# Expert phase: all column blocks from fetched token rows, none fetched for empty places

## What is computed

```python
scores = sigmoid(xt @ router_w)                # 384 tokens x 64 experts
idx = top 8 of 64, within 4 of 8 groups        # TOP_K = 8
w = scores[idx] / sum * 2.5
out = sum over the 8 chosen e of w_e * (silu(x @ w1[e]) * (x @ w3[e])) @ w2[e]
```

## Time and profile before

| | |
|---|---|
| median of 3 runs | 1401.55 us (1399.53 to 1402.01) |
| profiled execution | 1400.54 us |
| its span | 1398.7 us |
| mean granted TensorE clock | 0.997 |
| PE busy | 1363.8 us (98%) |
| DVE, ACT, POOL busy | 600.3, 392.6, 309.2 us |
| DMA traffic | 321.97 MB |
| expert weights, 198 loads of 1 MB | 207.6 MB |

### The profile page before, as it was taken

How to read it: one execution, slowest core, us unless ns; L and a number is a source line. 1 busy time by engine, 2 the same in 40 slices (tenths; PEclk the granted TensorE clock), 3 DMA queues, 4 the chain that set the end, 5 groups by cost and what they waited for, 6 DMA issues and landing times.

```text
span 1398.7 us, 20850 instructions
## 1 busy us (share of the span) xinstructions
PE 1363.8 (98%) x7808; PEld 958.6 (69%) x7808; DVE 600.3 (43%) x1347; ACT 392.6 (28%) x773; POOL 309.2 (22%) x247
## 2 busy tenths in 40 slices
PE   7999999999999999999999999999999999999996
PEld 2695898899988996788988875444455444444453
DVE  3467451885545477433321375232223322332224
ACT  3232221322554364323431241221121211221122
POOL 0431232243134552554233000000000000000001
PEclk9999999999999999999999999999999999999998
DMA  9540423123212428611135336899999999999992
GB/s 364 201 136 0 136 91 120 53 99 101 81 60 91 135 91 321 237 61 41 52 106 170 129 126 279 359 418 418 419 418 419 420 419 419 420 418 419 419 420 119
DMA packets 107376, 321.97 MB, mean 230 GB/s; under 512 B 9776, under 2 KB 69936, under 8 KB 78768
## 3 DMA queue, kind: packets, MB, share of 16 engines
q1 hardware_dynamic: 98416, 307.45, 56.6%
q0 software_dynamic: 2560, 10.49, 1.9%
q10 hardware_dynamic: 6336, 3.15, 0.8%
HBM read 316.93 MB, written 4.13 MB: 230 GB/s over the span
## 4 chain that ended last, share of the span: by engine, by line
PE 85%; DMA 10%; DVE 2%; ACT 1%; issue 1%; POOL 1%; SPq 0%; POOLq 0%; DVEq 0%
PE banks L647 21%; PE banks L614 20%; PE banks L2938 12%; PE banks L2989 7%; DMA w<-in_exp_w 7%; PE banks L2840 6%; PE banks L1054 3%; PE banks L2825 3%; PE banks L621 2%; PE banks L1207 1%; PE banks L886 1%; DMA ring<-in_ada_w 1%; PE banks L2833 1%; PE banks L766 1%; PE banks L698 1%
## 5 line engine op out<-in xcount | busy, mean ns | idle before, releaser
L2938 PE MATMUL banks<-w,xg 128*64 128x512 f32 (+1 forms) x1312 | 236.2, 594 | 0.9 <-DMA w<-in_exp_w 0.6
L2938 PEld LDWEIGHTS banks<-w,xg 128*64 128x64 f32 (+1 forms) x1312 | 72.0, 126 | 150.3 <-issue 124.0
L647 PE MATMUL banks<-hT,ring 128*128 128x192 f32 x792 | 137.6, 326 | 0.0
L3312 POOL DMA_INDIRECT fetched<-token_rows,row_of_place x32 | 30.4, 951 | 480.1 <-DVE row_of_place L3120 479.8
L647 PEld LDWEIGHTS banks<-hT,ring 128*128 128x128 f32 x792 | 129.6, 190 | 1.7 <-DMA ring<-in_w_in 0.4
L2989 PE MATMUL banks<-w,hidT 128*64 128x512 f32 (+1 forms) x656 | 122.0, 600 | 0.0
L2840 PE MATMUL banks<-y,selT 128*128 128x512 f32 x384 | 112.6, 415 | 0.0
L647 PE MATMUL banks<-x,ring 128*128 128x192 f32 x528 | 96.9, 327 | 0.9 <-ACT late L1383 0.9
L647 PE MATMUL banks<-x,combos 128*128 128x192 f32 x528 | 96.6, 326 | 0.0
L3130 DVE SCALAR_TENSOR_TENSOR hid<-banks,gslot,sil 128x256 f32<-128x256 f32 x33 | 16.0, 484 | 177.6 <-ACT sil L3024 176.9
L2840 PEld LDWEIGHTS banks<-y,selT 128*128 128x128 f32 x384 | 66.2, 189 | 35.4 <-issue 26.2
(11 more groups left out here) (483 smaller groups left out, 2055.7 us busy)
## 6 DMA issues: line engine op xcount, KB each, us to landing
w<-in_exp_w SPq DMA_DIRECT2D x198, 1024.0 KB, 17.2
ring<-in_w_in SPq DMA_DIRECT2D x46, 1024.0 KB, 5.2
ring<-in_ada_w SPq DMA_DIRECT2D x24, 1024.0 KB, 6.8
ring<-in_w_branch SPq DMA_DIRECT2D x8, 1024.0 KB, 6.2
ring<-in_w_out SPq DMA_DIRECT2D x4, 1024.0 KB, 6.2
arena<-in_sh_w SPq DMA_DIRECT2D x3, 1024.0 KB, 8.3
x<-in_x_sample SPq DMA_DIRECT2D x4, 512.0 KB, 8.7
arena<-in_t_last_layer SPq DMA_DIRECT2D x1, 1024.0 KB, 8.5
```

The source lines that it names most:

```text
L647: last = mm(out, lhsT=w[:, k, :], rhs=tokens[:, k, :], start=start and k == 0, stop=k == KD // 2 - 1, skip_group_check=not start)
L2938: ins = mm(ps[lo:hi, :], lhsT=xg[:, k, a_ * P + lo:a_ * P + hi], rhs=w13[:, a_, u, :, k, :], start=k == 0, stop=k == KD - 1)
L3312: nc.gpsimd.indirect_dma_start(fetched[:, a_, :], None, rows[:, :], bass.IndirectOffsetOnAxis(ap=row_of_place[:, 2 * a_:2 * a_ + 1], axis= ...
```

## The change

All eight column blocks come from fetched rows in every round but the first preparation, in which the first two blocks are still gathered. `token_rows`, `fetched` and a fetch are 1024 columns (4096 bytes a row). An empty place now has row 512, which is beyond the table's 384 rows: `turn_by` carries row - 512 and `rows_of_pair` adds 512. The indirect DMA is given a bound of 383 and told that a number beyond it is no error, so it fetches nothing for such a place. `fetched` is cleared once before the first fetch. `whole_rows` is one tile of 128 x 1024: GpSimd's add of a tile waits for the store of the one before, the third also for the planner's first table (X 2). TensorE waits for the fetches ahead of turned block 0, with 8 of 12 scatter matmuls (in the first round 12) before block 1, and one between each pair of the others.

```diff
-        sb("fetched", P, 2, D - FROM_ROWS),
+        sb("fetched", P, 2, D),
-        sb("whole_rows", P, NT, D - FROM_ROWS),
+        sb("whole_rows", P, D),
...
-    rows = nc.dram_tensor("token_rows", (T, D - FROM_ROWS), F32, kind="Internal").ap()
+    rows = nc.dram_tensor("token_rows", (T, D), F32, kind="Internal").ap()
...
-            if hi == 12:
+            if lo < hi == 12:
                 ins.then_inc(s_scat, 1)
...
                 elif a_:
-                    close_bank(gather(0, open_bank(GATHERS[0])))
-                    out = open_bank(GATHERS[1])
-                    gather(1, out, (0,))
-                    parts = (6, 10, 11, 12) if first else (6, 7, 10, 12)
+                    parts = (6, 12, 12, 12) if first else (8, 9, 10, 11)
                     if first:
+                        close_bank(gather(0, open_bank(GATHERS[0])))
                         scatter(1 - a_, *parts[0:2])
+                    else:
+                        scatter(1 - a_, 6, parts[0])
                     pe.wait_ge(s_fetched, 32 * q + 32)
-                    close_bank(turn_rows(1, out, (1,)))
                     if not first:
+                        close_bank(turn_rows(0, open_bank(GATHERS[0])))
                         scatter(1 - a_, *parts[0:2])
+                    close_bank(turn_rows(1, open_bank(GATHERS[1])))
+                    scatter(1 - a_, *parts[1:3])
                     close_bank(turn_rows(2, open_bank(GATHERS[2])))
-                    scatter(1 - a_, *parts[1:3])
+                    scatter(1 - a_, *parts[2:4])
                     close_bank(turn_rows(3, open_bank(GATHERS[3])))
                 if add:
-                    scatter(1 - a_, parts[2] if a_ else 6, 12)
+                    scatter(1 - a_, parts[3] if a_ else 6, 12)
...
-                    act.wait_ge(s_stored, 16 * NT)
+                    act.wait_ge(s_row_stored[NT - 1], 16)
...
-            v.tensor_copy(row_of_place[...], row_sum[...].to_broadcast([P, 2])).then_inc(s_rows, 1)
+            ts(row_of_place[...], row_sum[...].to_broadcast([P, 2]), float(NOWHERE), None, ALU.add
+               ).then_inc(s_rows, 1)
...
         for t in range(NT):
-            nc.gpsimd.tensor_tensor(whole_rows[:, t, :], h2[HI][:, t, FROM_ROWS:]..., h2[LO][:, t, FROM_ROWS:]..., ALU.add)
+            if t:
+                pool.wait_ge(s_row_stored[t - 1], 16)
+            if t == 2:
+                pool.wait_ge(s_read["dve"], read(0, "dve", ("X", 0, 2), "first"))
+            nc.gpsimd.tensor_tensor(whole_rows[:, :], h2[HI][:, t, :]..., h2[LO][:, t, :]..., ALU.add)
-        pool.wait_ge(s_stored, 16 * NT)
+        pool.wait_ge(s_filled, 1)
+        nc.gpsimd.memset(fetched[:, :, :], 0.0).then_inc(s_blank, 1)
+        pool.wait_ge(s_row_stored[NT - 1], 16)
+        pool.wait_ge(s_blank, 1)
...
-                    bass.IndirectOffsetOnAxis(ap=row_of_place[:, 2 * a_:2 * a_ + 1], axis=0)).then_inc(s_fetched, 16)
+                    bass.IndirectOffsetOnAxis(ap=row_of_place[:, 2 * a_:2 * a_ + 1], axis=0),
+                    bounds_check=T - 1, oob_is_err=False).then_inc(s_fetched, 16)
...
-            sp.dma_start(rows[t * P:(t + 1) * P, :], whole_rows[:, t, :]).then_inc(s_stored, 16)
+            sp.dma_start(rows[t * P:(t + 1) * P, :], whole_rows[:, :]).then_inc(s_row_stored[t], 16)
```

More of the change, by code:

```diff
@@ L31 @@
 TURN = GATED + 2
+NOWHERE = 512
 ROUTED = 2.5
@@ L2674, in _ @@
             expert_work["sync"](sp)
-FROM_ROWS = 3 * P
 def expert_tiles(ctx, nc):
@@ L2738, in experts @@
     row_of_place, fetched, whole_rows = (tiles[n] for n in ("row_of_place", "fetched", "whole_rows"))
-    staged = whole_rows[:, :, :].rearrange("p t n -> p (t n)")[:, 0:2 * NT * TURN].rearrange("p (a t c) -> p a t c", a=2, t=NT)
-    rows = nc.dram_tensor("token_rows", (T, D - FROM_ROWS), F32, kind="Internal").ap()
-    s_whole, s_stored = sem("whole_rows_ready"), sem("token_rows_stored")
+    staged = whole_rows[:, 0:2 * NT * TURN].rearrange("p (a t c) -> p a t c", a=2, t=NT)
+    rows = nc.dram_tensor("token_rows", (T, D), F32, kind="Internal").ap()
+    s_whole, s_row_stored = sem("whole_rows_ready"), [sem(f"token_rows_{t}_stored") for t in range(NT)]
     s_fetched, s_row = sem("rows_fetched"), sem("row_of_place_seen")
+    s_blank = sem("fetched_rows_blank")
     s_rowsum, s_rows = sem("row_of_place_summed"), sem("row_of_place_ready")
@@ L2819, in tensor_part, with gather @@
         mm = nc.tensor.matmul
-        def gather(j, out, ks=(0, 1)):
-            for i in ks:
+        def gather(j, out):
+            for i in range(2):
                 k = 2 * j + i
@@ L2827, in gather, with turn_rows @@
             return last
-        def turn_rows(j, out, ks=(0, 1)):
-            for i in ks:
-                at = (2 * j + i) * P - FROM_ROWS
+        def turn_rows(j, out):
+            for i in range(2):
+                at = (2 * j + i) * P
                 for a_ in range(2):
@@ L3119, in rows_of_pair @@
             dve.wait_ge(s_rowsum, 2 * q + a_ + 1)
-            v.tensor_copy(row_of_place[:, 2 * a_:2 * a_ + 2], row_sum[:, a_:a_ + 1].to_broadcast([P, 2])).then_inc(s_rows, 1)
+            ts(row_of_place[:, 2 * a_:2 * a_ + 2], row_sum[:, a_:a_ + 1].to_broadcast([P, 2]), float(NOWHERE), None, ALU.add
+               ).then_inc(s_rows, 1)
         def take(q, job, kind):
@@ L3219, in vector_part @@
         for t in range(NT):
-            ts(turn_by[:, t, GATED:TURN], iota[:, 2 * P:2 * P + 1].to_broadcast([P, 2]), float(t * P), None, ALU.add)
+            ts(turn_by[:, t, GATED:TURN], iota[:, 2 * P:2 * P + 1].to_broadcast([P, 2]), float(t * P - NOWHERE), None, ALU.add)
         link(v.tensor_copy(turn_by[:, :, 0:P], ident[:, None, :].to_broadcast([P, NT, P])))
@@ L3303, in gpsimd_part @@
         for t in range(NT):
-            nc.gpsimd.tensor_tensor(whole_rows[:, t, :], h2[HI][:, t, FROM_ROWS:].bitcast(F32), h2[LO][:, t, FROM_ROWS:].bitcast(F32),
+            if t:
+                pool.wait_ge(s_row_stored[t - 1], 16)
+            if t == 2:
+                pool.wait_ge(s_read["dve"], read(0, "dve", ("X", 0, 2), "first"))
+            nc.gpsimd.tensor_tensor(whole_rows[:, :], h2[HI][:, t, :].bitcast(F32), h2[LO][:, t, :].bitcast(F32),
                                     ALU.add).then_inc(s_whole, 1)
-        pool.wait_ge(s_stored, 16 * NT)
+        pool.wait_ge(s_filled, 1)
+        nc.gpsimd.memset(fetched[:, :, :], 0.0).then_inc(s_blank, 1)
+        pool.wait_ge(s_row_stored[NT - 1], 16)
+        pool.wait_ge(s_blank, 1)
         def fetch(q, kind):
```

## The result

| | before | after |
|---|---|---|
| median | 1401.32 us (4 runs) | 1415.88 us (4 runs, 1415.36 to 1418.5) |
| ratio | | 1.0113, 95% interval 1.0101 to 1.0126 |
| span of the profiled execution | 1398.7 us | 1414.4 us |
| its first refill | 877.35 | 885.03 |
| from there to the start of the last H | 492.2 us | 500.3 us |

Slower by 14.6 us between the medians (the ratio in the table is that of the record's own comparison; the quotient of the two medians is 1.0104). 1414.0 was forecast, with a range of 1402.0 to 1418.5. The three last lines of the table cut the span's 15.7 us in two: 7.7 us come before the weight stream begins, 8.1 us within it, and nothing behind it. The prediction had 1.9 us for the first part, and 12.5 - 1.3 = 11.2 us for the second. So the total is right and its parts aren't.

A forecast was written before the change was run, and what follows sets the result against it. The DMA engines were taken to bound the whole expert phase. Fetches +12.5, collision +1.9 and tail -1.3 gave +13.1 us on the profiled execution, 1413.6, forecast as a median of 1414.0 us, range 1402 to 1418.5.

The forecast's parts named there:

- What bounds: Expert phase: DMA engines bound every round at 26.2 GB/s each; PE's 1.57 us less a round gives the rounds nothing.
- The bytes: Fetches in the expert phase: 2865 rows of 4096 B, 11.73 MB, against 10.49 MB before.
- The pinned engine: Fetches: each row's engine follows from its partition, so the busiest engine gets 238 rows; +12.2 us, forecast's chance 0.48.
- the fetch term: Expert phase's weight stream: wider fetched rows on the busiest DMA engine lengthen it by 12.5 us.
- The tail: After the last weight wait PE runs 11.75 us without DMA waits; its shorter work counts there, -1.3 us (-1.6 to 0).
- The collision: Staging: GpSimd's second add blocks a VectorE planning step near 861 us, delaying the stream by 1.9 us (0 to 2.5).
- Staging and covers: Before the stream and in the first round: longer stores, third add, blanking and slower fetch are covered; cost 0, up to 1.
- (a): Fetches: rows spread evenly over the engines, whichever places are empty; +3.6 us in all, 1405; chance 0.16.
- (b): Fetches: places dealt out one by one, engine = place mod 16, busiest 208 rows; +8.1 us, 1409.6; chance 0.12.
- (c): Fetches: empty places are fetched at full width, +15.0 us for the fetches, 1417 in all; chance 0.08.
- (d): Fetches: paid by the row and not by the byte, so faster; -6.9 us, 1394.6; chance 0.08.
- (e): Staging and fetches: the add misses the planner, with rows spread evenly; +1.7 us, no change; chance 0.08.

The follow-up runs named there:

- late_lower: late_add with every fetch moving exactly 64 rows, to partitions 0 to 63 (output differs): 1416.32 us, 1.0107 of before.
- late_alternate: late_add with every fetch moving exactly 64 rows, to partitions 0 to 31 and 64 to 95 (output differs): 1396.47 us, 0.9966 of before.
- late_rev: late_add with the places of each quarter counted backwards in the second block: 1404.88 us, 1.0031 of before.
- late_add: The changed kernel with GpSimd's second add moved behind the planner's table and the blanking put after it: 1410.59 us, 1.0074 of before.
- late_full: late_add with empty places fetching row 0, so every fetch moves 128 rows of 4096 B: 1414.82 us, 1.0104 of before.
- collide: The kernel before with one more GpSimd add of 128x1024, started beside the planner's steps: 1408.32 us, 1.0056 of before.

## Why the prediction was right, point by point

**The total.** 1414.0 for 1415.88, and this is partly luck: two terms were off by 5.8 and 3.6 us, with opposite signs.

**What bounds.** Right. The DMA stream did, and its busiest engine at 26.2 GB/s. That PE's 1.57 us a round would bring nothing in the rounds held: rounds got longer with PE's work shorter. One sign that was named didn't come: GB/s fell, to 414 to 418 and in late_lower to 402, but the DMA share stayed at 1.01 and 1.00. Whether the less loaded engines stood idle or moved their packets more slowly is open.

**The bytes.** 2865 rows, 11.74 MB: right. The pinned engine, taken as the likeliest and argued only, is now shown by late_lower, late_alternate and late_rev. The round of about 32.3 us is 32.50 in the fullest ones and 32.12 on average.

**Size of the fetch term.** 12.5 was too much. From the first refill to the end of PE's last wait for w2 it is 1374.26 - 885.03 = 489.2 us after and 1357.67 - 877.35 = 480.3 us before: the term measured 8.9 us (8.6 in late_add, to 1367.61). Two checks place part of it. Where all engines are full (late_full) the same sum gives 15.0, and this stretch, to 1371.37, grew by 12.9. 0.25 MB of late_full's fetches, 0.6 us, were moved only after that wait, and the mean rate over the stretch was 417.4 GB/s before and 418.6 in late_full, which is another 1.3 us. The difference of late_full's and late_add's stretches to the last H, 5.2 us, is 2.3 more than 18 rows x 4096 B explain; that is open. Differences between two full kernels came out well: 19.8 us of stretch for 20 (late_alternate), 5.4 for 5.6 (late_rev).

**The tail.** -1.3 measured about -0.8. From the wait for w2 to the last H, PE needs 1385.17 - 1374.26 = 10.91 us now, 11.75 before, so 0.84 of the 1.57 us of shorter work came through. The step "PE runs 11.75 us to the next block without waiting for DMA" failed in the new kernel: with a shorter way from w2's wait to Y, PE meets w13's wait, for a load that ends 4 MB further in the queue, 10.0 us later at 419 GB/s, and it is that which ends at 1384.26. From the last H on nothing changed (29.1 us in both).

**The collision.** Place and mechanism right (an add landing on the planner, forecast for 861.0 to 863.5, was there from 861.88 to 864.24), price of the step right (2.2 for 1.9). What the prediction missed is what followed PE's gap here: 2.5 us idle, then some 13 us at 1.2 GHz. The term measured 7.7 us, not 1.9, and the first refill came at 885.03, not 879. This mis-sized term and the fetch term nearly cancelled.

**Staging and covers.** The third add waited for the table and was done at 873.5, the blanking at 875.2, both before they were wanted; the first round's second fetch took 11.76 us for 10.57, and PE waited 2.43 us for it, in time that the DMA engines were full. No cost, as forecast.

**Rivals.** (a), (b) and (c) are out: even rows by late_lower, place mod 16 by late_lower against late_alternate, full width for empty places by q0. (d), paying by the row, is out too: late_add fetches 30% fewer rows than the kernel before, without the collision, and is 0.74% slower; rounds follow the fullest engine's bytes. (e) is out, as the add did meet the planner, and rows aren't even.

## What to carry to other kernels

When a saturated DMA phase is sized, count bytes for each engine, not in all: a skipped row saves time only if its partition belongs to the engine that is fullest, and reordering places so that holes fall on all engines can gain time without removing a byte (5.7 us here). Before a helper engine's operation is moved, look at what chain of small steps of VectorE it will run beside, and add to the stop what TensorE may do after the idle gap (5 to 6 us for 2.2 here). And find how far the other engine's own pace lies below the bound before crediting a saving: in the kernel before it was 0.37 us a round.

## What the runs showed of the hardware that was not expected

- A gap of 2.5 us in PE's work at the planner (2.47 in the kernel after, 2.50 in collide) was followed by a granted clock of 0.50 (1.2 GHz) for about 13 us, although PE was busy again at once. The length of the gap isn't all that counts: at PE's first turned rows, gaps of 2.43 us (after), 2.45 (late_rev) and 2.66 (late_add) left the clock at 1.00, and 2.44 (late_full) and 2.53 (late_lower) were followed by 0.50 for some 3 us. What else decides is open. The two lines, of after and of late_full:

```profile
902.03 1.09 PE L2834 MATMUL banks<-ident,fetched 128*128 128x128 f32 x8 [2.43 <-DMA fetched<-token_rows,row_of_place]
```

```profile
894.00 3.01 PE L2834 MATMUL banks<-ident,fetched 128*128 128x128 f32 x12 [2.44 <-DMA fetched<-token_rows,row_of_place]
```

- A row number beyond an indirect DMA's bound moves no data (q0 11.74 MB for 2865 rows), and no other engine takes over what the fullest one has to do: 8.40 MB in 64 rows a fetch cost 19.9 us more on partitions 0 to 63 than on 0 to 31 with 64 to 95.
- A VectorE step with one input of 64x32 and a scalar for each partition (collide, L3181) lasted as long as the whole add as well, 2.42 us for 0.23, not only steps with two inputs.
